# Reciprocal softmax sums sent through DRAM in the second attention; near bias of every second softmax added by VectorE, and its outputs moved by ScalarE, in the first

## The reference

```
proj = rmsnorm(x) @ w_in                       # 11 parts: aq ak av ag | bq bk bv bg | iq ik iw
# first attention (A): 4 heads, two softmaxes each, chunk-causal
p  = softmax(q1 k1' * scale + bias) - lam * softmax(q2 k2' * scale + bias)
ao = rmsnorm(p @ v) * 0.8 * silu(ag)
# second attention (B): 8 heads, each query row sees only its 256 best keys
bo = softmax(q k' * scale + bias, chosen keys only) @ v * silu(bg)
out = rmsnorm(x + concat(ao, bo) @ w_out)
```

## Time and profile before

| | |
|---|---|
| median of 3 runs | 741.91 us (740.95 to 744.52) |
| profiled execution | 741.63 us, of which the trace spans 739.8 us |
| TensorE busy | 720.9 us (97%) |
| VectorE, GpSimd, ScalarE busy | 615.8, 366.1, 322.6 us |
| mean granted TensorE clock | 0.997 |
| first attention | from 241 to 366 us |
| second attention | from 519.7 to 643.5 us |

### The profile page before, as it was taken

One profiled execution on the slowest core, in us unless ns is written; L12 is line 12 of the kernel. 1 busy time (PEld: TensorE's weight loads), 2 busy tenths in 40 slices (PEclk: granted clock), 3 DMA queues, 4 the chain that ended last, 5 costly groups with the idle time before them and its releaser, 6 DMA issues.

```text
span 739.8 us, 12056 instructions
## 1 busy us (share of the span) xinstructions
PE 720.9 (97%) x4184; PEld 602.1 (81%) x4184; DVE 615.8 (83%) x1293; ACT 322.6 (44%) x723; POOL 366.1 (49%) x445
## 2 busy tenths in 40 slices
PE   8999999999999999999999999999899999999996
PEld 7757888888888898999888888888787878788886
DVE  5678999999997979898599999999689898646554
ACT  7547131131313666667531131314777767522222
POOL 5220222223556859771135555547999999612210
PEclk9999999999999999999999999999999999999999
DMA  7340211212220010113021112220010112312231
GB/s 282 113 143 20 57 44 44 57 43 57 68 62 1 1 43 2 43 31 100 16 70 44 47 39 57 53 76 1 30 44 10 50 46 89 127 57 95 78 113 58
DMA packets 24564, 44.58 MB, mean 60 GB/s; under 512 B 3076, under 2 KB 10936, under 8 KB 24376
## 3 DMA queue, kind: packets, MB, share of 16 engines
q1 hardware_dynamic: 23336, 42.76, 19.5%
q10 hardware_dynamic: 1168, 1.05, 0.4%
HBM read 35.40 MB, written 6.57 MB: 57 GB/s over the span
## 4 chain that ended last, share of the span: by engine, by line
PE 85%; DVE 5%; POOL 4%; issue 2%; DMA 2%; ACT 1%; SPq 0%; POOLq 0%; DVEq 0%; ACTq 0%
PE psum L1273 41%; PE psum L1494 12%; PE psum L1356 5%; PE psum L1368 4%; PE psum L1334 4%; PE psum L1337 4%; PE psum L1383 3%; PE psum L1228 3%; PE psum L1211 3%; PE psum L1193 2%; PE psum L1165 2%; DMA xs<-in_x 1%; PE psum L1341 1%; PE psum L1340 1%; DVE probs L1761 1%
## 5 line engine op out<-in xcount | busy, mean ns | idle before, releaser
L609 POOL TENSOR_TENSOR w_lo<-w_raw,w_hi 128x512 fp32r<-128x512 f32 x60 | 77.5, 1294 | 215.5 <-ACT w_hi L807 215.2
L1640 DVE MATCH_REPLACE8 score<-top,score 128x640 f32<-128x640 f32 (+5 forms) x176 | 157.4, 906 | 0.0
L1635 DVE MAX8 top<-score 128x8 f32<-128x640 f32 (+5 forms) x176 | 148.7, 910 | 1.1
L807 ACT ACTIVATE w_hi<-w_raw 128x512 fp32r<-128x512 f32 x60 | 37.4, 629 | 209.8 <-PE psum L1273 206.8
L983 ACT ACTIVATE probs<-psum,small 128x384 f32<-128x384 f32 (+7 forms) x128 | 94.8, 741 | 38.4 <-DVE small L1700 30.0
L1273 PE MATMUL psum<-big_hi,w_hi 128*128 128x512 f32 x256 | 99.7, 389 | 0.0
L1273 PE MATMUL psum<-big_hi,w_lo 128*128 128x512 f32 x256 | 99.6, 389 | 0.0
L1273 PE MATMUL psum<-big_lo,w_hi 128*128 128x512 f32 x256 | 99.6, 389 | 0.0
L1273 PE MATMUL psum<-w_hi,big_hi 128*128 128x512 f32 x192 | 74.7, 389 | 0.0
L1273 PE MATMUL psum<-w_lo,big_hi 128*128 128x512 f32 x192 | 74.7, 389 | 0.0
L1273 PE MATMUL psum<-w_hi,big_lo 128*128 128x512 f32 x192 | 74.7, 389 | 0.0
(11 more groups left out here) (195 smaller groups left out, 1630.7 us busy)
## 6 DMA issues: line engine op xcount, KB each, us to landing
w_raw<-in_w_in SPq DMA_DIRECT2D x62, 256.0 KB, 2.6
xs<-in_x SPq DMA_DIRECT2D x8, 512.0 KB, 7.0
k_high_twice<-k_high_twice SPq DMA_DIRECT2D x16, 256.0 KB, 3.7
xres<-in_x SPq DMA_DIRECT2D x8, 512.0 KB, 4.3
out_y<-y_out SPq DMA_DIRECT2D x8, 384.0 KB, 2.9
w_tail<-in_w_out SPq DMA_DIRECT2D x10, 256.0 KB, 2.6
bias_scratch<-bias_row SPq DMA_DIRECT2D x1, 2304.0 KB
bias<-bias_scratch SPq DMA_DIRECT2D x12, 128.0 KB, 3.0
```

The source lines that it names most:

```text
L609: pool.tensor_tensor(lo[:, 0:cols], w_staged(n)[:, 0:cols], hi[:, 0:cols].bitcast(f32), ALU.subtract).then_inc(w_lo_made, 1)
L807: act.activation(w_parts(n)[0][:, 0:cols], w_staged(n)[:, 0:cols], ACT.Copy).then_inc(w_hi_made, 1)
L1635: ins = dve.max(top8[:, i - SEL0, :], sc)
L1640: ins = dve.match_replace(sc, top8[:, i - SEL0, :], sc, TAKEN)
```

## The change

1. In A the bias of m = 1 is no longer added by TensorE. VectorE does it, as in B: the extreme over the far columns first (`far_min`), then `soften` over the last 224 columns, where the bias comes from a copy kept in `near_high` (four more loads of 128 KB, `keep_bias`). `SAME = 32`: the first 32 of the 256 band columns have no bias of their own, so `soften` and GpSimd's `near` take 224 columns.
2. In A the output of a step is moved out of PSUM by ScalarE (`move_out`), not by VectorE (`finishA`).
3. In B `share`, `turn_shares` and `scale_gate` go. `invert` signals SP, which stores the 256 reciprocals of a step to DRAM (`store_sums`) and loads them back as rows spread over 64 partitions each (`load_shares`, two DMAs). VectorE multiplies output and gate first (`finishB`) and the result by the shares four steps later (`scale_mix`). In steps whose probabilities are turned in two pieces (tiles 0 to 3) `invert` stands behind the softmax work of the loop, in the others ahead of it.
4. The scores of B have five banks, and TensorE turns two pieces ahead of the next scores in every step.
5. SP's list in B now goes step by step. The key copies and w_out loads stand inside it.

```diff
+SAME = 32
-        S_BANKS, BACK_BANK, O_BANK, T_BANK = (4, 4), 4, 5, 6
+        S_BANKS, O_BANK, T_BANK = (4, 5), 5, 6
+        def near_width(i):
+            return P * (i + 1) if i < SEL0 else BAND - SAME
+        SHARE_LAG = 4
...
# SP, second attention
-            for b in range(1, BLOCKS):
-                copy_keys(1, b)
-                for n in range(CHUNKS + 3 + (0, 1, 3)[b - 1], CHUNKS + 3 + (1, 3, 6)[b - 1]):
-                    load_chunk(n)
-            for n in range(CHUNKS + 9, CHUNKS + 2 * DB):
+            def store_sums(s):
+                c = 2 * s % 8
+                sp.wait_ge(sums_inverted, s + 1)
+                if s >= 4:
+                    sp.wait_ge(shares_loaded[s % 4], 32 * (s // 4))
+                sp.dma_start(bass.AP(sum_rows, s % 4 * 2 * P, [[1, P], [P, 2]]), rinv[:, c:c + 2],
+                             allow_slow_non_contiguous=True
+                             ).then_inc(shares_stored[s % 4], 16)
+            def load_shares(s):
+                sp.wait_ge(shares_stored[s % 4], 16 * (s // 4 + 1))
+                if s >= 4:
+                    sp.wait_ge(mixB_scaled, s - 3)
+                for m in range(2):
+                    sp.dma_start(shares[m * HEAD:(m + 1) * HEAD, s % 4, :],
+                                 bass.AP(sum_rows, (s % 4 * 2 + m) * P, [[0, HEAD], [1, P]])
+                                 ).then_inc(shares_loaded[s % 4], 16)
+            for s in range(STEPS):
+                b, piece = divmod(s, TILES)
+                store_sums(s)
+                if s >= 1:
+                    load_shares(s - 1)
+                if piece == 5 and b + 1 < BLOCKS:
+                    copy_keys(1, b + 1)
+                for k, (after, split_at) in enumerate(OUT_TIMES):
+                    if s == after * TILES + split_at + 2:
+                        load_chunk(CHUNKS + 3 + k)
+            load_shares(STEPS - 1)
+            for n in range(CHUNKS + 3 + sum(b * TILES + piece + 2 < STEPS for b, piece in OUT_TIMES),
+                           CHUNKS + 2 * DB):
                 load_chunk(n)
...
# TensorE
-                    banded = ph == 0 and near < c + w
+                    banded = ph == 0 and m == 0 and near < c + w
-            def turn_shares(s):
-                pe.wait_ge(shares_made, s + 1)
-                pe.wait_ge(gate_scaled, s)
-                pe.transpose(bank(BACK_BANK)[:, 0:P], shares.rearrange("p m d -> p (m d)"), ident[:, :]
-                             ).then_inc(shares_turned, 1)
...
# ScalarE, first attention, at the head of step s for step s - 2
+            def move_out(s):
+                act.wait_ge(combined, s + 1)
+                act.wait_ge(pv_done, quads_through(0, s))
...
+                act.activation(o_tmp[:, s % 4, :], bank(O_BANK)[:, 0:P], ACT.Copy,
+                               scale=rinv[:, 2 * s % 8:2 * s % 8 + 1]).then_inc(o_moved, 1)
...
# VectorE, first attention
                 if s + 1 < STEPS:
                     far_min(0, s + 1, 1)
-            finishA(STEPS - 2)
-            finishA(STEPS - 1)
+                    soften(0, s + 1, 1)
...
# VectorE, second attention
+            def scale_mix(s):
+                b, i = place_of(1, s)
+                g = mixB[:, b, i * P:(i + 1) * P]
+                dve.wait_ge(o_moved, STEPS + s + 1)
+                dve.wait_ge(shares_loaded[s % 4], 32 * (s // 4 + 1))
+                dve.tensor_tensor(g, g, shares[:, s % 4, :], ALU.mult).then_inc(mixB_scaled, 1)
...
-                if 1 <= s <= STEPS:
-                    invert(1, s - 1)
-                    share(s - 1)
+                few = len(qs) == 2
+                if s >= SHARE_LAG and not few:
+                    scale_mix(s - SHARE_LAG)
                 if s >= 2:
                     finishB(s - 2)
                 turned(1, qs)
+                if qs and not few:
+                    invert(1, s - 1)
                 if s + 1 < STEPS:
                     for m in range(2):
                         far_min(1, s + 1, m)
                         soften(1, s + 1, m)
-                if 1 <= s <= STEPS:
-                    scale_gate(s - 1)
+                if few:
+                    invert(1, s - 1)
+                    if s >= SHARE_LAG:
+                        scale_mix(s - SHARE_LAG)
```

More of the change, by code:

```diff
@@ L149, in build @@
     w_tail, _ = place("w_tail", [P, 2, WIDTH], f32, at=w_hi_at + 2 * ROW)
-    shares, _ = place("shares", [P, 2, HEAD], f32, at=o_tmp_at)
+    shares, _ = place("shares", [P, 4, P], f32, at=o_tmp_at)
     lam4, _ = place("lam4", [P, 4, HEAD], f32, at=mask_at + 4096)
@@ L266, in build @@
         o_moved = sem("o_moved")
-        shares_made = sem("shares_made")
-        shares_turned = sem("shares_turned")
-        gate_scaled = sem("gate_scaled")
+        sums_inverted = sem("sums_inverted")
+        shares_stored = [sem(f"shares_stored{r}") for r in range(4)]
+        shares_loaded = [sem(f"shares_loaded{r}") for r in range(4)]
+        mixB_scaled = sem("mixB_scaled")
         o_squared = sem("o_squared")
@@ L537, in _ @@
                 load_bias(h)
+            for h in range(3):
+                keep_bias(h)
             for n in range(DB + SW, Q0 - 2):
@@ L547, in _ @@
             copy_keys(0, 2)
+            sp.wait_ge(max_ready, 2 * TILES)
+            keep_bias(3)
             load_chunk(Q0 + 3)
@@ L753, in near @@
                 end = score_off[i] + P * (i + 1)
-                pool.tensor_tensor(near_slot(k), bias[:, A_HEADS + 2 * b + m, :], mask[:, end - BAND:end], ALU.add
-                                   ).then_inc(near_made, 1)
+                pool.tensor_tensor(near_slot(k)[:, SAME:BAND], bias[:, A_HEADS + 2 * b + m, SAME:BAND],
+                                   mask[:, end - BAND + SAME:end], ALU.add).then_inc(near_made, 1)
             pool.wait_ge(mask_made, len(CHOSEN_ORDER))
@@ L1440, in attend_chosen @@
                     qs = quads[1, t] if t >= 0 else []
-                    long = len(qs) == 4
-                    for quad in qs[0:1 if long else 2]:
+                    for quad in qs[0:2]:
                         turn(1, t, quad)
@@ L1679, in _ @@
             dve.memset(bias[0:CHUNK, 0:A_HEADS, BAND - CHUNK:BAND], MASKED).then_inc(bias_masked, 1)
+            dve.wait_ge(bias_kept[0], 16 * 3)
+            link(dve.memset(near_high[0:CHUNK, :, BAND - CHUNK:BAND], MASKED))
             dve.memset(mask_bias[:, 0:1], MASK_BIAS).then_inc(mask_bias_made, 1)
@@ L1695, in far_min @@
                 i = place_of(ph, s)[1]
-                far = P * (i + 1) - min(BAND, P * (i + 1))
+                far = P * (i + 1) - near_width(i)
                 u = (ph * STEPS + s) * 2 + m
                 dve.wait_ge(s_ready, u + 1)
-                if ph == 0:
+                if ph == 0 and m == 0:
                     dve.tensor_reduce(negmax[:, u % 4:u % 4 + 1], score_of(u, 0, P * (i + 1)), AX.X, ALU.min
                                       ).then_inc(max_ready, 1)
+                elif far and ph == 0:
+                    far_done[u] = later(dve.tensor_reduce(farmin[:, u % 4:u % 4 + 1], score_of(u, 0, far), AX.X,
+                                                          ALU.min))
                 elif far:
@@ L1722, in soften @@
                     dve.wait_ge(exp_done, u - 3)
-                added = bias[:, h, BAND - w:BAND]
+                added = near_high[:, b % 3, :] if ph == 0 else bias[:, A_HEADS + 2 * b + m, :]
+                added = added[:, BAND - w:BAND]
                 if u - 2 * STEPS in near_of:
@@ L1735, in invert @@
                 dve.wait_ge(exp_done, 2 * (ph * STEPS + s) + 2)
-                inverted[ph, s] = later(dve.reciprocal(rinv[:, c:c + 2], rsum[:, c:c + 2]))
+                if ph == 0:
+                    if s >= 4:
+                        dve.wait_ge(o_moved, s - 3)
+                    inverted[ph, s] = later(dve.reciprocal(rinv[:, c:c + 2], rsum[:, c:c + 2]))
+                    return
+                if s >= 4:
+                    dve.wait_ge(shares_stored[s % 4], 16 * (s // 4))
+                dve.reciprocal(rinv[:, c:c + 2], rsum[:, c:c + 2]).then_inc(sums_inverted, 1)
             def turned(ph, quads):
@@ L1790, in _ @@
                 combine(s)
+                if s == 3 * TILES - 2:
+                    dve.wait_ge(bias_kept[1], 16)
+                    link(dve.memset(near_high[0:CHUNK, 0, BAND - CHUNK:BAND], MASKED))
                 if s + 1 < STEPS:
                     far_min(0, s + 1, 1)
-            finishA(STEPS - 2)
-            finishA(STEPS - 1)
+                    soften(0, s + 1, 1)
             select(1, SEL0 + 1)
@@ L1810, in _ @@
                               ALU.not_equal, ALU.mult).then_inc(last_mask_made, 1)
-            def share(s):
-                c = 2 * s % 8
-                dve.wait_ge(dve_own, inverted[1, s])
-                if s >= 1:
-                    dve.wait_ge(shares_turned, s)
-                dve.tensor_copy(shares[:, :, :], rinv[:, c:c + 2].unsqueeze(2).broadcast_to([P, 2, HEAD])
```

(14 more changed lines are left out.)

43 lines of the change are left out of this document (19 added, 24 removed).

## The result

The changed kernel takes **834.38 us** (median of four runs, 831.66 to 837.35); the kernel before took 741.93 beside it. The ratio is 1.1244, 95% interval 1.12 to 1.1288. The prediction was 755, with a range of 744 to 763: the direction holds, the size does not. The profiled execution has a span of 833.9 us.

The account below looks back on a forecast made before the run. The prediction took TensorE, busy 720.9 of 739.8 us, as the bound, with key copies barely hidden at the second attention's block starts. Terms -2.0 + 18.2 + 2.5 - 8.2 + 2.8 = +13.3 us gave 755 us, range 744 to 763.

Parts of the forecast that it names:

- 3.0 us, the price of the bias load: End of second attention: wait for step 31's store of sums to land, taken as 3.0 us from the bias load.
- the latter are late by no more than a step, and VectorE wants them four steps later, so I cost that at nothing: Second attention: loads of shares queued behind the waiting store would not hold up VectorE; costed at nothing.
- late copies and late shares: Rival, second attention: `scale_mix` blocked or waiting for loads makes VectorE the bound, 0.4 us more a step, 768 us; chance 0.05.
- Key copies behind the sums, +18.2: Second attention, three block boundaries: SP issues key copies only after step 5's reciprocal and store, so TensorE waits; +18.2 us.
- The clock, bounds 0 to 4.5: Second attention: three waits of 6 us may lower TensorE's granted clock; +2.5 us, bounds nothing to 4.5.
- What B gains, -8.2: Second attention: TensorE loses a transposition a step, VectorE the share copies; 2.05 us a block, -8.2, bounds -4 and -16.
- A, -2.0, bounds -8.6 to +3: First attention: TensorE loses 72 bias matmuls, VectorE's softmax work grows; -2.0 us, bounds -8.6 and +3.
- block 3's 2.1 us: First attention, block 3: VectorE has room, so its 2.1 us are won for the most part; other blocks about nothing.
- The end of B, +2.8: End of second attention: last w_out pieces load and split late, so the output projection's first half tile waits; +2.8 us, bounds 0 and 5.
- `scale_mix` blocked by GpSimd: Second attention: each `scale_mix` could wait out a GpSimd pass of 1.29 us; not used in the sum.
- worst case of 41 us: Second attention: all 32 `scale_mix` each wait out a GpSimd pass of 1.29 us, 41 us of VectorE's time.

Follow-up runs that it names:

- two_rows: Changed kernel with the store of the sums as two pieces of 512 bytes taken from the identity: 763.42 us, ratio 1.029 to the kernel before.
- pairs: Changed kernel with the store of the sums in 128 pieces of 8 bytes instead of 256 of 4: 771.17 us, ratio 1.0392 to the kernel before.
- no_transfers: Changed kernel without the stores and loads of the reciprocal sums, shares filled once with ones: 741.22 us, ratio 0.9976 to the kernel before.
- a_alone: Kernel before with the change in the first attention only, the second attention left as before: 743.73 us, ratio 1.0013.
- a_last: Kernel before with the first attention's change in its last block only: 741.79 us, ratio 1.0003.
- two_rows_keys: two_rows with the second attention's key copies issued by ScalarE instead of SP: 745.65 us, ratio 1.0047 to the kernel before.
- lag: Changed kernel loading shares of step s - 3, not s - 1, behind the store of step s, and scaling six steps later: 828.64 us, ratio 1.1138.
- lag_pairs: lag with the store of the sums in 128 pieces of 8 bytes: 770.26 us, ratio 1.0385 to the kernel before.
- lag_keys: lag with the second attention's key copies issued by ScalarE: 805.39 us, ratio 1.0855 to the kernel before.
- one_column: Changed kernel storing only the first head's sums, 128 pieces of 4 bytes, both loads from that row: 834.27 us, ratio 1.121 to the kernel before.

## Why the prediction was wrong

*The step that failed.* "3.0 us, the price of the bias load" for the store's landing, and with it "the latter are late by no more than a step, and VectorE wants them four steps later, so I cost that at nothing". The store lands after 7.9 us, more than two steps of 3.6, the loads behind it are late as well, and VectorE stands still for the shares for 59.6 us. The bias load moves rows of 1 KB; no DMA of the kernel before moves pieces of 4 bytes, and the value should have had a bound on the far side. The 834.38 less two_rows' 763.42, **71 us**, hang on this term, and all but 8 of them went with pieces of 8 bytes (pairs, 771.17). The price of nothing was too low even with a quick store: in pairs, whose landing of 3.5 us is near the 3.0 assumed, VectorE still waits 10.3 us for shares, in two_rows 2.7. The rival "late copies and late shares" named the right mechanism, VectorE standing still in `scale_mix`, but gave it 13 us and a chance of 0.05: it priced 0.4 us more a step, where a ring of 19 us for three steps makes it 2.6.

*Key copies behind the sums, +18.2, with the clock +2.5.* Right in mechanism and place. In two_rows GpSimd's last memset for block 1 ends at 542.55 us, VectorE's reciprocal of step 5 runs at 545.84, and SP issues the copies at 547.50. With a store that costs little, the copies' place is worth 17.8 us, 12.1 of waits and about 4.9 of clock, where the sum had 20.7. In the changed kernel the three waits are 25.6 us in all, 8.3 more than in two_rows. The copies land after 6.0, 5.3 and 4.7 us there (3.7 at block 1 of two_rows), and the loads in front of them wait 0.2 to 1.5 us for the landing of step 4's store; together that is most of the 8.3.

*The clock, bounds 0 to 4.5.* Just above the bounds in two_rows (4.85, for three waits). In the changed kernel the granted clock is 0.83 over B (0.99 before), and TensorE's list, shorter by 32 turns, is busy for 135.32 us where it was 113.54 in no_transfers: 21.8 us, since it now waits again and again and not three times. This is a part of the 71 us.

*What B gains, -8.2.* Wrong. no_transfers, with all gains of A and B and no transfer, is 0.7 us faster by the medians and at most 2.9 by its interval. The -4 that I took as the least was for TensorE's turns alone; by the chain GpSimd's list took even that. I had read GpSimd's 26.95 and 27.39 us of 29 as "near as well", and then cost the gain by VectorE. It weighs by itself: the sum without the gains of A and B is 765, and two_rows, where the store costs little, takes 763.42, already just above the range.

*A, -2.0, bounds -8.6 to +3.* The bounds held (a_alone: +1.0 by its ratio, interval -0.4 to +2.4 us; B begins 0.8 us later in the changed kernel, not 1 to 3 earlier). The value did not: that block 3's 2.1 us are won is refuted by a_last.

*The end of B, +2.8.* The times in the sum give 651.4 - 648.3 = 3.1. In two_rows TensorE waits 2.9 us for the last split of `w_out`, as worked out, in the changed kernel 9.0 in two waits.

*`scale_mix` blocked by GpSimd.* The nine instances read above agree with the Trainium skill (SBUF — State Buffer, "Who interferes with whom"), by which a VectorE instruction with two SBUF inputs contends with a GpSimd instruction that reads SBUF, and the later one is blocked. The sum over 32 is far from the worst case of 41 us, since few of them meet a whole pass: 13.1 us (mean 418 ns) in the changed kernel, 15.2 (mean 512 ns) in no_transfers, where GpSimd is busier. Both lie under the 0.7 us each that the prediction allowed for.

Put together: 741.9 (before) - 0.7 (all gains) + 4.4 (transfers of two pieces, the end of B included; two_rows_keys) + 17.8 (key copies) + 71 (pieces of 4 bytes) = 834.4. Each term but the first is the difference of two runs that follow each other, so the sum must close; how large a term would be with the others in place no run says.

## What to carry to other kernels

Price a new transfer by the size of its pieces: a transposing store of single 4-byte values is no small transfer, and here it held up whatever stood behind it, so look for any row with pieces of that size, and without one give the term an upper bound of several steps. Before costing what an engine's relief is worth, ask which engine's list comes next: leaving the suspect work out altogether shows what the whole idea can win (here 0.4% at most) before anyone tunes it. A copy that the next block waits for should not stand in an in-order list behind something that is made at the end of this block.

## What the hardware showed unexpectedly

A store from 128 partitions to DRAM in 256 pieces of 4 bytes landed after 7.0 to 10.3 us, and nine with 128 such pieces after 7.66 to 10.27; in pieces of 8 bytes the medians were 4.0 (256) and 3.5 (128). With such stores ahead of them, loads on the same queue had a median of 8.5 us (lag) instead of 3.0 (lag_pairs), and 256 KB copies on ScalarE's queue 7.7 (lag_keys; 9.0 on SP's in lag, 3.4 in lag_pairs). With half the pieces of 4 bytes the followers were less late, 4.1 us for the loads and 5.9 for the copies (one_column), but the kernel took the same time. SP's issue was held at times as well: two loads behind a store took 2.32 us at 575.12 in the changed kernel, where 1.08 at 582.20 was usual. Why 4 bytes are so much dearer than 8 no run here tells.
